# Layer 1's gated unit kept in the accumulation banks, half of its output projection as seven block products, and a later start for GpSimd's sums

## What is computed

```
# layer 1, glu_out
y = gelu(y)                                     # 256 x 2048
ya, yb = split(y @ w_glu + b_glu, 2, axis=-1)   # w_glu: 2048 x 4096
out = ((ya * sigmoid(yb)) * silu(g)) @ w_out    # w_out: 2048 x 1024
x = layernorm(alpha * x + gt * out, ln_g, ln_b)
# second block
hn = rms_norm(x, norm1_g)
proj = hn @ w_in                                # w_in: 1024 x 5120
```

## Time and profile before

| | us |
|---|---|
| median of three runs | 1625.85 |
| lowest, highest | 1624.64, 1627.67 |
| the profiled execution, its own time | 1624.87 |
| span of the profiled execution | 1623.1 |
| busy: PE / PEld | 1528.4 / 1135.9 |
| busy: DVE / ACT / POOL | 870.3 / 389.2 / 449.2 |

### The profile page before, as it was taken

One profiled execution on the slowest core, in us unless ns is written; L12 is line 12 of the kernel. 1 busy time (PEld: TensorE's weight loads), 2 busy tenths in 40 slices (PEclk: granted clock), 3 DMA queues, 4 the chain that ended last, 5 costly groups with the idle time before them and its releaser, 6 DMA issues.

```text
span 1623.1 us, 25140 instructions
## 1 busy us (share of the span) xinstructions
PE 1528.4 (94%) x10208; PEld 1135.9 (70%) x10208; DVE 870.3 (54%) x1671; ACT 389.2 (24%) x920; POOL 449.2 (28%) x360
## 2 busy tenths in 40 slices
PE   4999989999999999999999898899999989999999
PEld 3455556666645578889887787774788764788887
DVE  5889944554589977574785524522533322233312
ACT  1223243342312223133322100000223441311100
POOL 4023330000003313000018866722576200000264
PEclk9999999999999999999999999999999999999999
DMA  9846770230496545767773534443543123444451
GB/s 322 230 156 195 246 247 1 53 113 5 174 309 205 195 143 173 258 248 251 292 277 121 193 130 154 155 155 130 193 170 141 52 104 104 140 150 147 147 179 68
DMA packets 172345, 272.94 MB, mean 168 GB/s; under 512 B 51149, under 2 KB 85048, under 8 KB 170952
## 3 DMA queue, kind: packets, MB, share of 16 engines
q1 hardware_dynamic: 145840, 201.08, 36.7%
q0 software_dynamic: 16512, 42.49, 8.1%
q10 hardware_dynamic: 9880, 27.78, 4.7%
HBM read 228.26 MB, written 42.99 MB: 167 GB/s over the span
## 4 chain that ended last, share of the span: by engine, by line
PE 83%; DVE 10%; issue 2%; ACT 2%; DMA 2%; POOL 0%; DVEq 0%; ACTq 0%; POOLq 0%
PE bank L488 78%; PE bank L491 5%; DMA memory<-in_w_mod 1%; DVE memory L2419 1%; DVE memory L2421 1%; DVE memory L2416 1%; DVE memory L2414 1%; DVE memory L2329 0%; DMA memory<-in_s_log_dt 0%; DVE memory L2330 0%; DVE memory L2336 0%; DVE memory L2333 0%; DMA memory<-mc_scratch 0%; DVE memory L2377 0%; DVE memory L2375 0%
## 5 line engine op out<-in xcount | busy, mean ns | idle before, releaser
L488 PE MATMUL bank<-memory 128*128 128x256 f32 (+9 forms) x9348 | 1433.9, 356 | 51.5 <-issue 9.4
L488 PEld LDWEIGHTS bank<-memory 128*128 128x128 f32 (+4 forms) x9348 | 1038.2, 166 | 407.2 <-issue 268.1
L2667 POOL TENSOR_TENSOR memory<-memory 128x1024 f32<-128x1024 f32 (+1 forms) x32 | 75.9, 2373 | 442.9 <-DMA memory<-in_w_ffn_down 254.1
L2628 POOL DMA_DIRECT2D mc_scratch<-memory x32 | 28.0, 875 | 505.7 <-DVE memory L2052 447.9
L491 PE MATMUL bank<-memory 128*128 128x128 f32 (+1 forms) x860 | 116.3, 279 | 39.2 <-DVE memory L2421 16.4
L491 PEld LDWEIGHTS bank<-memory 128*128 128x128 f32 (+1 forms) x860 | 99.4, 143 | 75.6 <-issue 31.9
L2634 POOL DMA_DIRECT2D k_scratch<-memory x128 | 76.2, 630 | 14.5 <-ACT memory L1372 14.1
L2670 POOL TENSOR_TENSOR memory<-memory 128x1024 f32<-128x1024 f32 (+1 forms) x32 | 79.9, 2497 | 0.0
L2669 POOL TENSOR_TENSOR memory<-memory 128x1024 f32<-128x1024 f32 (+1 forms) x32 | 78.1, 2440 | 2.5
L2672 POOL TENSOR_TENSOR memory<-memory 128x1024 f32<-128x1024 f32 (+1 forms) x32 | 76.8, 2400 | 2.5
L2537 DVE SCALAR_TENSOR_TENSOR memory<-bank,memory 128x255 f32<-128x255 f32 x44 | 21.0, 478 | 98.8 <-ACT memory L1791 98.8
(11 more groups left out here) (290 smaller groups left out, 1147.5 us busy)
## 6 DMA issues: line engine op xcount, KB each, us to landing
memory<-in_s_w_glu SPq DMA_DIRECT2D x16, 2048.0 KB, 8.3
memory<-in_w_mod SPq DMA_DIRECT2D x12, 2048.0 KB, 14.1
memory<-in_w_ffn_up SPq DMA_DIRECT2D x22, 1024.0 KB, 7.0
memory<-in_w_in SPq DMA_DIRECT2D x10, 2048.0 KB, 7.9
mc_scratch<-memory POOLq DMA_DIRECT2D x32, 512.0 KB, 4.3
mb_scratch<-memory ACTq DMA_DIRECT2D x32, 512.0 KB, 3.6
memory<-mb_scratch SPq DMA_DIRECT2D x32, 512.0 KB, 7.4
memory<-mc_scratch POOLq DMA_DIRECT2D x32, 512.0 KB, 6.4
```

Source lines behind the costliest of these rows:

```text
L488: return nc.tensor.matmul(o, l, r, start=start, stop=stop, skip_group_check=free)
L2628: pool.dma_start(mc_dram[u], over(mc[:, u % 3, GS:GS + 1], (144, 8), (1, P))).then_inc(*S.up("mc_out%d" % (u % 3), u, by=16))
L2667: nc.gpsimd.tensor_tensor(t1, b12, b11, ALU.subtract).then_inc(*S.up("w_sum", (key, 1)))
```

## The change

1. **The banks.** `glu_out` becomes `seven_joined`, which writes its results back into the banks (bank 0 and 1, or 4 and 5) and not to memory. Bias, sigmoid and the last multiplication read them there; each VectorE instruction has at most one operand in memory. Bias and `gs` for `ya` move up behind the first half of each ct, and only the bias of `yb`, the sigmoid and one multiplication for each jh are left behind the second half. `yb` and one part buffer go. A bank is now released to TensorE by `gated` or `z`, not by the join.
2. **out1, n = 0** becomes two units of seven products (56 matmuls of 128x256 for 32 of 128x512). This adds eight VectorE instructions for left sums (`out1_sums(0)` behind the gating of ct 3, `out1_sums(1)` behind the last `z`), eight of GpSimd for weight sums, three copies on ScalarE and a join on VectorE. `z_turned(3)` stands between the fourth and the fifth product of the first unit. n = 1 stays plain, in banks 6 and 7 in place of 2 and 3.
3. **GpSimd** waits, before the weight sums of in2, for `hn` of the second half of the tokens.

```diff
@@ weights
-                load(("out1", n, kh), ..., (KD, 512), ("out1_k", (n, kh)))
+                load(("out1", n, kh), ..., (KD, 512),
+                     ("out1_k", (n, kh)) if n else ("product", (("out1", n, kh), 4)))
@@ TensorE
                 product(b[1][:, T:2 * T], s[:, 1], t2, False, end).then_inc(*S.up("product", (key, 6)))
+                if between is not None:
+                    z_turned(between)
...
-                    b = [bank(pe, ("glu", ct, half, i), [("glu_x", (ct, half))], 4 * half + i) for i in range(4)]
+                    b = [bank(pe, ("glu", ct, half, i), [("z", (ct, 1)) if half else ("gated", (ct, 1))], 4 * half + i) for i in range(4)]
...
+            b = [bank(pe, ("out1", 0, i), [("res1_a", (0, 1))], i) for i in range(4)]
+            for kh in range(2):
+                for jh in range(2):
+                    pe.wait_ge(*S.at("zT", (2 * kh + 1, jh)))
+                seven_raw(b, ("out1", 0, kh), 4, zT, 8 * kh, kh == 0, kh == 1)
+                pe.wait_ge(*S.at("out1_sum", kh))
+                seven_sums(b, ("out1", 0, kh), 4, zT, 8 * kh, glu_sums[:, kh], kh == 0, kh == 1, None if kh else 3)
+            for t in range(2):
+                b = bank(pe, ("out1", 1, t), [("res1_a", (1, t))], 6 + t)
@@ ScalarE
-                    A(yb[:, jh, :], yb[:, jh, :], ACT.Sigmoid).then_inc(*S.up("sig", (ct, jh)))
+                    A(at_bank("glu", ct, 1, jh), at_bank("glu", ct, 1, jh), ACT.Sigmoid).then_inc(*S.up("sig", (ct, jh)))
...
             gated_turned(3)
+            seven_parts(("out1", 0, 1), (4, 0), ("out1", 0), (3, 1))
@@ VectorE
+            def out1_sums(kh):
+                for ct in (2 * kh, 2 * kh + 1):
+                    for jh in range(2):
+                        dve.wait_ge(*S.at("zT", (ct, jh)))
+                dve.wait_ge(*S.at("product", (("glu", 3, 1, kh), 4)))
+                left_sums(glu_sums[:, kh], ...)
+            def seven_joined(key, places, ct, half):
...
+                link(tt(b[0][:, lo], b[0][:, hi], u1, ALU.add))
+                dve.wait_ge(*S.at("glu_a5", (ct, half)))
+                link(tt(b[1][:, hi], b[1][:, hi], u1, ALU.add))
+                link(tt(s5, b[1][:, hi], a5, ALU.add))
+                dve.wait_ge(*S.at("glu_w7", (ct, half)))
+                link(tt(b[0][:, hi], b[2][:, hi], s5, ALU.add))
+                link(tt(x1, b[1][:, hi], w7, ALU.add))
+                link(tt(b[1][:, hi], b[2][:, lo], s5, ALU.add))
+                dve.wait_ge(*S.at("product", (key, 4)))
+                tt(b[1][:, lo], b[3][:, lo], x1, ALU.add).then_inc(*S.up("glu_x", (ct, half)))
...
+                seven_joined(("glu", ct, 0, 1), ("glu", ct, 0), ct, 0)
+                for jh in range(2):
+                    b = at_bank("glu", ct, 0, jh)
+                    link(tt(b, b, glu_bias[:, ct % 2, 0, :], ALU.add))
+                    tt(ya[:, jh, :], b, gs[:, ct, jh, :], ALU.mult).then_inc(*S.up("gated", (ct, jh)))
+                if ct == 3:
+                    out1_sums(0)
+                seven_joined(("glu", ct, 1, 1), ("glu", ct, 1), ct, 1)
+                for jh in range(2):
+                    b = at_bank("glu", ct, 1, jh)
+                    tt(b, b, glu_bias[:, ct % 2, 1, :], ALU.add).then_inc(*S.up("biased", (ct, jh)))
+                for jh in range(2):
+                    tt(ya[:, jh, :], at_bank("glu", ct, 1, jh), ya[:, jh, :], ALU.mult).then_inc(*S.up("z", (ct, jh)))
+            out1_sums(1)
+            seven_joined(("out1", 0, 1), ("out1", 0), 4, 0)
@@ GpSimd
+            for kh in range(2):
+                w_sums(("out1", 0, kh), 4, ("glu", 3, 1, kh))
+            pool.wait_ge(*S.at("hn", (0, 1)))
             for n, ct in enumerate(IN2_ORDER):
                 w_sums(("in2", ct), 4, ("in2", IN2_ORDER[n - 2]) if n >= 2 else None)
```

90 lines of the change are left out of this document (34 added, 56 removed).

## The result

| | before | after |
|---|---|---|
| median, us | 1626.76 | 1598.81 |
| lowest to highest of 4 runs | 1624.64 to 1628.64 | 1598.16 to 1600.22 |
| span of the profiled execution | 1623.1 | 1596.4 |
| busy PE / DVE / POOL | 1528.4 / 870.3 / 449.2 | 1516.4 / 848.2 / 461.8 |

The ratio is 0.983 with a 95% interval of 0.9813 to 0.9847. The forecast was 1600.0. The change made the kernel 28 us faster in this series; in a second series the same kernel had 1600.54 against 1625.28, 24.7 us. So the size is known to a few us only, and the stretches of the traces are needed to say more.

What follows compares the result with a forecast made beforehand. TensorE bounds the kernel (83% of the last chain), VectorE counting only where TensorE waits. Terms -24.8 - 4.2 - 1.8 + 4.5 + 0.5 = -25.8 took 1624.87 to 1599.1, median 1600.0; own range 1598 to 1602, full range 1594.0 to 1604.5.

Steps and rivals of the forecast that it cites:

- a term of -24.8: Gated product: three waits of 5.46 us for `z`, each with 2.5 to 3.0 of slow work, vanish; 24.8 us saved.
- The bound from the reading rows: Gated product: bank-writing instructions take as long as bank-reading ones, 0.42 us for 256 columns and 0.69 for 512.
- a late `z`: Rival, ct 3 ahead of out1: bank writes nearer 2.83 us than 0.69, +3 to +5, 1604; chance 0.07.
- banks that do not help: Rival, gated product: GpSimd still holds up bank instructions, 1.7 us past the reader three times plus clock falls, 1614; chance 0.03.
- seven times the time: Rival "slower", gated product: writing banks takes seven times as long, 27.5 us of waits and slow work; chance 0.03.
- -4.2: out1: seven-product units save 3.4 us of matmuls, and the 0.83 wait for turned `z` goes, -0.8.
- The pile-up: in2: VectorE's four `in_sum` rows alternate with GpSimd's 2.8 us instructions, TensorE waits four times; +4.5 us.
- no pile-up: Rival, in2: VectorE's four sums slip in between GpSimd's instructions, so the hold only helps; 1595.0, chance 0.18.
- The `qk` norms: Transposes of q and k after in2: norms run against GpSimd as before, given +0.5 us, ends -1.5 and +1.5.
- the page's +5.1: in2: by the skill page's strict port turns, the three pairs cost 0.6 us more than forecast; total 1600.6.
- the rival that put a fall there: Rival, in2: dense gaps make TensorE's clock fall once, costing 2.5 to 3.0 us; 1602.8, chance 0.17.
- The sign that I had named against myself: Behind the end of out1: a clock under 1.00 was listed among the signs that the forecast is wrong.

Runs made afterwards that it cites:

- part 1 alone: Kernel before plus only the bank results and the moved bias and gate; out1 plain, GpSimd not made to wait for `hn`: 1600.36 us, ratio 0.9833 to 0.9862.
- the last experiment but one: Changed kernel with results in banks, but bias and gate of each first half put back behind the second half's join: 1630.43 us, ratio 1.0021 to 1.0042.
- the order without banks: Changed kernel with the new order of VectorE's operations, but the gated unit's results written to memory tiles again: 1606.07 us, ratio 0.9866 to 0.9892.
- without the hold: Changed kernel minus GpSimd's wait for `hn` before in2's weight sums: 1597.28 us, ratio 0.9810 to 0.9835.
- with the moved one: Changed kernel with GpSimd waiting only from in2's second column on, for VectorE's `in_sum` 4: 1596.21 us, in a second series 1594.90.
- the later hold: Changed kernel with all of GpSimd's in2 weight sums waiting for VectorE's `in_sum` 4 instead of `hn`: 1601.36 us, ratio 0.9840 to 0.9879.

## Why the prediction was right

**Part 1.** The three waits of 5.46 us and the slow work behind them are gone. From 924.65 to the last unit's end at 1060.58 it is 135.9 us, 160.4 before: -24.5 for a term of -24.8, and part 1 alone gave -24.9 up to the first turning of `hn`. The bound from the reading rows was the right end: bank-writing rows take 0.43 for 256 columns and 0.69 for 512, so the rivals that rested on slow writes (a late `z`, banks that do not help, seven times the time) fall. The argument that nothing is lost by the later release of the banks was true, but I had called it nothing without a price; the last experiment but one puts the cover's price at some 30 us.

What the prediction did not ask is which half of part 1 earns the time. It reasoned from the short rows on banks. The kernel with the order and without the banks has rows of 2.6 to 2.7 us on the mean and still no wait at the three turnings, so the moved bias and gate give them back by themselves, with 0.6 us to spare at the one shown. What the banks are shown to add is that margin (`z` comes 3.2 us behind the unit and not 11.5) and 6.0 us at the fourth turning, where part 2 had shortened the cover. The number was right; the credit given to the banks was not.

**Part 2.** out1 took 52.3 us from the last unit's end to its own end, 56.85 before: -4.5 for -4.2. `z` of ct 3 came 3.2 us behind the unit and not 5.4. The step that was off: `out1_sums(0)` ended at 1057.42, 3.2 ahead of the end and not 0.8, as the first of its four instructions took 0.69; VectorE had caught up. It cost nothing either way.

**Part 3.** The turning came 8.7 us behind the end of out1 (9.1 forecast), the norm's last pass took 1.28. The pile-up happened as told: `in_sum` 1, 3, 2 and 4 ended 4.9, 7.6, 10.4 and 13.2 us behind the turning, where the sum had 5.0, 7.8, 10.6 and 13.4. It cost 5.2 and not 4.5: the sum stopped at product 3 of column 0, the one that needs `in_sum` 4, which started 13.25 behind the turning for a forecast of 13.4; behind it the trace has a gap of 0.26 ahead of 1146.06, for L2465, and 10.90 us for 48 records where 80 took 17.50 before, 0.4 too much. The last 0.2 are not placed. VectorE's joins, which I had not counted, are slowed as well: L2472, with both operands in memory, took 1.80 us for 256 columns at 1135.50. (A slip that changes nothing: 17.50 / 10 is 1.75, not 1.73.) The `qk` norms cost 0.15 and not 0.5. The rival "no pile-up" is wrong; the kernels without the hold and with the moved one show that the two streams and not the turned tiles make the rows long.

On the pair of ports, the Trainium skill (SBUF — State Buffer, section "SBUF: two separate sides") has whoever starts first hold it for the whole instruction. The turn-taking is in the trace, one for one, but a pair took 2.8 us again and not 3.0: by strict turns `in_sum` 4 would have ended near 14.0, and it ended at 13.2. That the whole stretch, +5.2, came out near the page's +5.1 is by the gaps behind, not by longer pairs.

**The clock.** In both traces of the changed kernel the granted clock stayed at 1.00 through the four gaps of in2: eight records take 1.97 to 1.99 us there. Two other traces have the same gaps, and in these it fell. Here are 4 us behind the first gap in the order without banks and in the banks without order (length, TensorE's busy time, clock, DMA share, GB/s):

```profile
1135.00:1139.00 4.00, 3.89 (x10) 0.57 0.55 174
```

```profile
1158.00:1162.00 4.00, 4.00 (x11) 0.62 0.56 183
```

The fall cost nothing: 24 records took 7.45 us in one piece, where the changed kernel has 24 records and two waits in 7.46 (1126.63 to 1134.09), and the way to q and k is 26.22 and 26.20, as in the changed kernel. The slower work filled time in which TensorE would have waited for VectorE's next sum. So the rival that put a fall there was right about the fall in two of four traces and wrong about its price, 2.5 to 3.0 us. The sign that I had named against myself, a clock under 1.00 behind the end of out1, is a poor one: it can come and leave the time as it is. What the Trainium skill says of small gaps between groups of matmuls, that they make the clock swing (TensorE: Matmul & The Clock Gate, section "A second HAM failure mode: psum-queue depth-cycling"), agrees with these two traces and not with the other two: in the changed kernel TensorE was busy for 1.78 of the 4 us from 1124 to 1128, and the clock held.

```profile
1124.00:1128.00 4.00, 1.78 (x8) 1.00 0.99 314
```

**The sum.** -25.8 against -25.9 from the start of the product to the end. The median moved by 28.0 and in the second series by 24.7. What the traces show to vary between executions is what lies ahead of the product (its first sums started between 870.4 and 872.8 us in the ten traces that have the wait) and the clock at its start, 1.3 us; together they can hold a difference of that size, but the executions without a trace cannot be split.

## What to carry to other kernels

Look first at what stands between the end of a product and the tile that TensorE waits for, and move ahead whatever can be done earlier: here this alone took three waits of 5.46 us away. Then look at the place. Where VectorE and GpSimd both worked in memory, each long instruction of VectorE's took as long as one of GpSimd's beside it (2.6 to 2.8 us over 512 columns); with one operand in an accumulation bank it took 0.69. But such a bank stays taken until VectorE has read it, so see when TensorE wants it back. A wait that keeps two engines apart at one place puts them together at the next: look who runs when the held one is let go, and put the hold behind the last short list that matters. And wait for the part that the next product reads, not for the last of a list.

## What the runs showed that I had not expected

Behind a wait of 2.13 us the clock fell in some executions and not in others. The wait stands at the start of the product in ten traces, behind the same work. In seven of them the granted clock was 0.57 to 0.70 in the 4 us from 872 and the 248 records took 55.48 us in place of 54.16 (the kernel before, the changed kernel); in three (the kernel before, the changed kernel once, the banks without order) it was 1.00. Here are the stretches of the changed kernel and of the banks alone (length, TensorE's busy time, clock, DMA share, GB/s):

```profile
868.00:872.00 4.00, 1.87 (x9) 1.00 0.51 187
872.00:876.00 4.00, 4.00 (x20) 1.00 0.00 0
```

```profile
868.00:872.00 4.00, 1.87 (x9) 1.00 0.75 202
872.00:876.00 4.00, 4.00 (x13) 0.57 0.00 0
```

TensorE did the same in both, so a trace without a fall is no proof that a wait is free. The DMA share in the 4 us from 868 does not sort the traces (0.51, 0.70 and 0.91 without a fall, 0.50 to 0.95 with one), nor does the moment at which the wait ended (870.65 without, 870.67 with one). The wait of 2.22 us in in2 behaves alike: a fall behind it in two traces and none in two. What decides it is open. In the part of the kernel that is cut into stretches here, the nine waits of 4.30 us and more (three before, one in the order without banks, four in the banks without order, one with the later hold) were each followed by a lowered clock, at a price of 1.7 to 3.1 us.
